# First mixer of a two-block network: order of the weight queue, place of the filters, one accumulating bank for the modulation, low ranks side by side

## The reference

```python
mod_x = split((silu(c) @ w_ada + b_ada), 6)          # 6 x 1024, and mod_c from c_ctx
def project(h, mod):
    p = modulate(rmsnorm(h, norm_mix_g), mod[0], mod[1]) @ w_in
    q, k, v, g, a_f, a_b, hy = split(p)
    la_f = log_sigmoid(a_f @ gla_wa_f + gla_ba_f) / 16   # a_f, a_b: 16 columns each
    la_b = log_sigmoid(a_b @ gla_wa_b + gla_ba_b) / 16
gla_c = project(ctx, mod_c)                          # the context gives states only
gla_x = project(x, mod_x)
_, s_f, s_b = gla_bidir(*gla_c)
o_x = gla_bidir(*gla_x, s_f, s_b)
filt = hyena_filters(hy_w1, hy_b1, hy_w2, hy_b2, hy_w3, hy_freq)
y = concat([gla_out(o_x, g), hyena(hy, hy_conv_w, hy_conv_b, filt, hy_bias)]) @ w_out
x = x + mod_x[2] * y
x = x + mod_x[5] * expert_choice_moe(...)            # experts: 201 MB of weights
```

## Time and profile before

| | |
|---|---|
| median of 3 executions | 1749.27 us (1746.94 to 1749.31) |
| profiled execution | 1747.91 us, span 1746.0 us |
| TensorE busy | 1501.8 us (86%), granted clock 0.936 |
| VectorE, ScalarE busy | 513.7 us (29%), 332.2 us (19%) |
| DMA | 493.45 MB, mean 283 GB/s |

### The profile page before, as it was taken

How to read it: one execution, slowest core, us unless ns; L and a number is a source line. 1 busy time by engine, 2 the same in 40 slices (tenths; PEclk the granted TensorE clock), 3 DMA queues, 4 the chain that set the end, 5 groups by cost and what they waited for, 6 DMA issues and landing times.

```text
span 1746.0 us, 18568 instructions
## 1 busy us (share of the span) xinstructions
PE 1501.8 (86%) x7642; PEld 834.0 (48%) x7642; DVE 513.7 (29%) x1103; ACT 332.2 (19%) x693; POOL 0.2 (0%) x4
## 2 busy tenths in 40 slices
PE   6999998775665666589999899999899998999997
PEld 3567776331221211156778443343567785434434
DVE  6312742100111100015653322121347624221213
ACT  1423211100000000102331322111223323122112
POOL 0000000000000000000000000000000000000000
PEclk9999998888888878889999899999999999999998
DMA  9325528799999999982331699999214216999980
GB/s 387 141 76 203 204 108 374 306 427 427 427 427 429 427 427 429 426 347 99 114 113 55 267 411 394 390 388 391 111 59 183 97 49 241 402 394 402 370 358 26
DMA packets 35309, 493.45 MB, mean 283 GB/s; under 512 B 3920, under 2 KB 4304, under 8 KB 4688
## 3 DMA queue, kind: packets, MB, share of 16 engines
q1 hardware_dynamic: 34784, 491.62, 68.7%
q10 hardware_dynamic: 432, 0.52, 0.1%
HBM read 491.08 MB, written 1.05 MB: 282 GB/s over the span
## 4 chain that ended last, share of the span: by engine, by line
PE 72%; DMA 21%; DVE 4%; ACT 1%; issue 1%; DVEq 0%; ACTq 0%
PE PS L543 22%; DMA A<-ring_d 21%; PE PS L1343 13%; PE PS L1366 7%; PE PS L856 3%; PE PS L1328 3%; PE PS L1216 3%; PE PS L1381 3%; PE PS L548 3%; PE PS L1007 2%; PE PS L1205 1%; PE PS L1042 1%; PE PS L613 1%; PE PS L1169 1%; PE PS L555 1%
## 5 line engine op out<-in xcount | busy, mean ns | idle before, releaser
L543 PE MATMUL PS<-A 128*128 128x256 f32 (+7 forms) x1744 | 424.7, 402 | 7.5 <-ACT A L2363 3.8
L856 PE MATMUL PS<-A 128*32 128x512 f32 x1536 | 237.7, 754 | 154.6 <-DMA A<-ring_d 154.6
L543 PEld LDWEIGHTS PS<-A 128*128 128x128 f32 (+2 forms) x1744 | 313.5, 197 | 107.2 <-issue 59.5
L1343 PE MATMUL PS<-A 128*64 128x512 f32 x1024 | 226.8, 595 | 0.2
L856 PEld LDWEIGHTS PS<-A 128*32 128x32 f32 x1536 | 52.6, 124 | 329.3 <-issue 249.9
L1343 PEld LDWEIGHTS PS<-A 128*64 128x64 f32 x1024 | 71.5, 137 | 133.8 <-issue 132.3
L1366 PE MATMUL PS<-A 128*64 128x512 f32 x512 | 116.9, 598 | 0.0
L1849 DVE TENSOR_TENSOR A<-A,PS 128x512 f32<-128x512 f32 x8 | 5.5, 690 | 344.3 <-PE PS L856 344.3
L548 PE MATMUL PS<-A 128*128 128x128 f32 (+1 forms) x462 | 73.1, 290 | 27.6 <-DVE A L1849 7.1
L548 PEld LDWEIGHTS PS<-A 128*128 128x128 f32 (+1 forms) x462 | 55.8, 150 | 71.5 <-issue 43.1
L2250 DVE TENSOR_TENSOR A<-A,PS 128x256 f32<-128x256 f32 x32 | 13.5, 423 | 225.2 <-ACT A L2782 225.2
(11 more groups left out here) (337 smaller groups left out, 1255.6 us busy)
## 6 DMA issues: line engine op xcount, KB each, us to landing
A<-ring_d SPq DMA_DIRECT2D x228, 2048.0 KB, 12.2
A<-ring_d SPq DMA_DIRECT2D x2, 1312.0 KB, 16.1
A<-ring_d SPq DMA_DIRECT2D x2, 1280.0 KB, 16.6
A<-xT_d SPq DMA_DIRECT2D x2, 1024.0 KB, 9.0
A<-p_d SPq DMA_DIRECT2D x1, 1278.5 KB, 5.5
A<-p_d SPq DMA_DIRECT2D x1, 1232.0 KB, 24.6
A<-pf_d SPq DMA_DIRECT2D x2, 512.0 KB, 13.2
A<-cT_d SPq DMA_DIRECT2D x1, 1024.0 KB, 19.7
```

The lines of the kernel that those rows point to most:

```text
L543: ins = g.matmul(out, l, r, start=n == 0, stop=n == len(pairs) - 1)
L856: ins = g.matmul(ps[32 * e:32 * e + 32, :], rows_of(kk, e), wv[:, kk % 2, e, :], start=kk == 0, stop=kk == 7)
L1343: ins = g.matmul(ps[64 * s:64 * s + 64, :], XS2[u % 2][:, kk, c:c + 64], wv[:, kk % 4, s, :], start=kk == 0, stop=kk == 7)
```

## The change

It does this:
- **Order.** `FILTERS` is split. `SETUP` holds the sine network's first part, the norms, `ada 0` to `3`, `mod 0`, `hm`, and `hz` at its end; the eight `ht` and two `sp` go into the merged strand behind `g 3`. `GLA_IN` begins with `k 1 0`, `k 1 1`. `LATE` has `ada 4` to `11`, and the shares are other.
- **New order** that results: w1 w2 xsq xsum xs, ada 0, csq csum cs, ada 1 to 3, mod 0, hm 1, hm 0, hz, k 1 0, k 1 1, a, gates, k 0 0, k 0 1, v 1 0, b 0 1, ada 4, v 1 1, b 1 1, kt 0 1, ada 5, q 0, st 0 1, q 1, kt 1 1, v 0 0, b 0 0, ada 6, st 1 1, v 0 1, kt 0 0, g 0, ada 7, b 1 0, st 0 0, g 1 to 3, qk 0, kt 1 0, ada 8, ht 0 0 to 1 0, scr 0 0, ht 1 1, st 1 0, ht 1 2, scr 0 1, ht 1 3, sp 0, ada 9, sp 1, hy 0, qk 1, hy 1, ada 10, hy 2, scr 1 0, hy 3, scr 1 1, o 0, ut 0, cv 0, ada 11, o 1, hy 4, osum, hy 5, hy 6, ob 0, ob 1, mod 1, hy 7, ic 0, ut 1, cv 1, hy 8 to 11, ic 1, wr, out 0.
- **Queue.** The constants come in three parts (0.42, 0.56 and 0.51 MB) at three places; the 1 MB of positions is replaced by two small tables that VectorE adds by broadcast; `w3`, decay, and the transform tables are issued later, those of ScalarE's queue now on SP's. The mixer's 20 blocks use three buffers throughout.
- **Modulation.** All blocks of a group add up in one held bank: the coefficients `SCP` are taken at a shifting place, so that block n lands in rows of its own. One copy and four column matmuls end a group.
- **Low ranks.** `a` multiplies both sources in one step, in columns 0 to 48 and 64 to 112 of the array.
- **Smaller.** The sine network's second layer makes 128 rows, and ScalarE a copy with a sign, in place of `wf`; `hm` has 3 rows on ScalarE and 5 on VectorE; the first two operations of `cv` on VectorE are made whole.

The core of the diff:

```diff
-FILTERS = [("w1",), ("w2",), ("hz",), ("xsq",), ("xsum",), ("wf",)] + [("ht", odd, od) for odd in range(2) for od in range(4)] \
-    + [("xs",), ("csq",), ("ada", 0), ("ada", 1), ("csum",), ("cs",), ("sp", 0), ("ada", 2), ("ada", 3),
-       ("mod", 0), ("sp", 1), ("hm", 1), ("hm", 0)]
+SETUP = [("w1",), ("w2",), ("xsq",), ("xsum",), ("xs",), ("ada", 0), ("csq",), ("csum",), ("cs",), ("ada", 1), ("ada", 2), ("ada", 3),
+         ("mod", 0), ("hm", 1), ("hm", 0), ("hz",)]
+FILTERS = [("ht", odd, od) for odd in range(2) for od in range(4)] + [("sp", 0), ("sp", 1)]
-GLA_IN = [("a", 1), ("a", 0), ("gates",)] + [("k", s, j) for s in (1, 0) for j in range(2)]
+GLA_IN = [("k", 1, 0), ("k", 1, 1), ("a",), ("gates",), ("k", 0, 0), ("k", 0, 1)]
-LATE = [("ada", b) for b in range(6, 12)] + [("mod", 1)]
-MIX1 = FILTERS + GLA_IN + merged((REST + CONV, 1), (gla_direction(0), 0.65), (gla_direction(1) + GLA_OUT, 0.65), (LATE, 0.15)) \
+LATE = [("ada", b) for b in range(4, 12)] + [("mod", 1)]
+MIX1 = SETUP + GLA_IN + merged((REST + FILTERS + CONV, 1), (gla_direction(0), 1), (gla_direction(1) + GLA_OUT, 0.8), (LATE, 0.16)) \
...
             def ada(blk):
-                if blk in (0, 4):
-                    fresh("mod", blk // 4 > 0, hold=True)
+                n = int(blk > 3)
+                first, last = ((0, 3), (4, 11))[n]
...
+                c = 14 - 2 * (blk - first)
                 for kk in range(2):
                     for q in range(4):
-                        ins = g.matmul(ps[32 * q:32 * q + 32, :], SCP[:, 2 * q + kk, :], wv[:, 2 * q + kk, :], start=kk == 0, stop=kk == 1)
+                        ins = g.matmul(bank("ada", n)[32 * q:32 * q + 32, :], SCP[:, 2 * q + kk, c:c + 32], wv[:, 2 * q + kk, :],
+                                       start=blk == first and kk == 0, stop=blk == last and kk == 1, skip_group_check=True)
-                if blk not in (0, 4):
-                    mod_columns(blk - 1)
...
-            def a_(s):
-                across(("a", s), w_ab, 0, 49, rows_ready(s))
+            def a_():
+                ps = fresh("a")
+                g.wait_ge(*at("late"))
+                rows_ready(1)
+                rows_ready(0)
+                for k in range(8):
+                    for s, r in ((1, slice(0, 49)), (0, slice(64, 113))):
+                        ins = g.matmul(ps[r, 0:256], w_ab[:, k, :], (H, CH)[s][:, k, :], start=k == 0, stop=k == 7)
...
             def cv(o):
+                v.tensor_tensor(YS[:, 0:2, :], E, XO, ALU.add).then_inc(*out())
+                settle()
+                v.tensor_tensor(YS[:, 2:4, :], E, XO, ALU.subtract).then_inc(*out("cv", o, 0))
...
         def sync(q):
+            constants(1, "in0", "p1")
+            q.dma_start(X, xT_d.rearrange("p (k t) -> p k t", k=8)).then_inc(*land("in2", "in2"))
             for i, (key, n) in enumerate(order):
                 if i == 1:
                     q.dma_start(M, cT_d.rearrange("p (k t) -> p k t", k=8)).then_inc(*land("in3", "ctx"))
+                elif i == 4:
+                    constants(2, "in10", "late")
+                elif i == 5:
+                    q.wait_ge(*at("ch", "n", 1))
+                    tables("w3", w3, "in1", "w3")
+                    q.wait_ge(*at("h", "n", 1))
+                    tables("decay", decay, "in7", "decay")
+                elif i == 6:
+                    constants(0, "in12", "perm")
+                    tables("masks", masks.bitcast(F32), "in6", "masks")
+                    q.dma_start(CE, pf_d[:, PF["CE"][0]:PF["CE"][0] + 128]).then_inc(*land("in4", "CE"))
+                    tables("CF", CF, "in11", "CF")
+                    tables("IC", IC, "in5", "IC")
```

More of the change, by code:

```diff
@@ L46 @@
 ])
-PF, PFN = columns([("decay", 1024), ("w3", 2048), ("CE", 128), ("CF", 512), ("IC", 512), ("mF", 128), ("mB", 128)])
+PF, PFN = columns([("decay", 1024), ("w3", 1024), ("CE", 128), ("CF", 512), ("IC", 512), ("masks", 256)])
 CAP = 128
 CAPX = 64
-COST = dict(ada=4, hy=8, ht=2, sp=8, ut=2, cv=8, ic=2, q=8, k=8, v=16, g=8, csum=8, xsum=8, a=8, b=20, kt=14, st=20, qk=16, scr=4, o=8, osum=10,
+COST = dict(ada=4, hy=8, ht=2, sp=8, ut=2, cv=8, ic=2, q=8, k=8, v=16, g=8, csum=8, xsum=8, a=12, b=20, kt=14, st=20, qk=16, scr=4, o=8, osum=10,
             kx=8, cq=16, ckv=8, cqsum=2, kvsum=1, kpe=2, vm=2, qa=4, km=2, qb=2, ca=16, cb=2, kir=2, vc=13, bkr=1, ix=1, tk=2,
             da=16, db=2, sc=3, sm=3, tr=3, pv=3)
-AFTER = {("ada", 6): ("hy", 0), ("b", 1, 1): ("v", 1, 1), ("o", 0): ("scr", 0, 1)}
+AFTER = {("hy", 0): ("sp", 1), ("b", 1, 1): ("v", 1, 1), ("o", 0): ("scr", 0, 1)}
 for _d in range(2):
@@ L177, with mixer_slots @@
 YE_SLOT, MT_SLOT = 7, 8
-SLOTS = [0, 1, 2, 3] * 2 + [0, 1, 2] * 4 + [4, 5, 6, YE_SLOT, 0, 1, 2, MT_SLOT] + [4, 5, 6, 0, 1, 2] * 14 + [4, 5, 6, 0] \
+def mixer_slots():
+    use = {}
+    for n, (kind, *a) in enumerate(MIX1):
+        key = dict(ada=lambda: ("ada", a[0]), q=lambda: ("qk",), k=lambda: ("qk",), v=lambda: ("v",), g=lambda: ("g",),
+                   hy=lambda: ("hy", a[0] // 4), out=lambda: ("out", a[0] // 2)).get(kind, lambda: None)()
+        if key:
+            use[key] = (use.get(key, (n, n))[0], n)
+    through, slots = [-1] * NM, []
+    for first, last in sorted(use.values()):
+        x = through.index(min(through))
+        assert through[x] < first
+        through[x] = last
+        slots.append(x)
+    in_order = sorted(range(NM), key=lambda x: through[x])
+    return [in_order.index(x) for x in slots]
+SLOTS = mixer_slots() + [4, 5, 6, YE_SLOT, 0, 1, 2, MT_SLOT] + [4, 5, 6, 0, 1, 2] * 14 + [4, 5, 6, 0] \
     + ([1, 2, 4, 5, 0] * 2 + [1, 2, 4, 5, 0, 6] * 8) * 2
@@ L593, in sp @@
                         ins.then_inc(*full("sp", o, x))
[L595 to L601, removed]
             def ada(blk):
-                if blk in (0, 4):
-                    fresh("mod", blk // 4 > 0, hold=True)
+                n = int(blk > 3)
+                first, last = ((0, 3), (4, 11))[n]
                 w, i = weights("ada", blk)
                 wv = w.rearrange("p (k n) -> p k n", k=8)
-                ps = fresh("ada", blk)
+                if blk == first:
+                    fresh("ada", n, hold=True)
+                c = 14 - 2 * (blk - first)
                 g.wait_ge(*at("scp"))
@@ L1563, in xsq @@
                 v.wait_ge(*at("in2"))
-                v.wait_ge(*at("places"))
-                v.tensor_tensor(X, X, T, ALU.add).then_inc(*out("xa"))
+                for k, place, shape in ((0, p1("posr", 4, 4, 1), [128, 4, 4, 64]), (4, p1("posc", 4, 1, 64), [128, 4, 4, 64])):
+                    rows = X[:, k:k + 4, :].rearrange("p k (r c) -> p k r c", r=4)
+                    ins = v.tensor_tensor(rows, rows, bc(place, shape), ALU.add)
+                    ins.then_inc(*(out("xa") if k else out()))
                 settle()
@@ L1630, in ic, with a_ @@
                 v.tensor_tensor(dst, UF[:, m, :], gate_, ALU.mult).then_inc(*out("ic", o, m))
-            def a_(s):
-                full("a", s)
-                v.tensor_scalar(aF[0:49, s, :], bank("a", s)[0:49, 0:256], p1("aone")[0:49, :], None, ALU.add).then_inc(*out("a", s))
+            def a_():
+                v.wait_ge(*at("late"))
+                full("a")
+                for s, r in ((1, slice(0, 49)), (0, slice(64, 113))):
+                    v.tensor_scalar(aF[0:49, s, :], bank("a")[r, 0:256], p1("aone")[r, :], None, ALU.add).then_inc(*out("a", s))
+                note("dve", "a")
             def gates():
@@ L2393, in ada @@
             def ada(blk):
-                full("ada", blk)
-                if blk >= 2:
-                    full("columns", blk - 2)
-                s.activation(ROW[blk % 2], bank("ada", blk), ACT.Copy).then_inc(*out("ada", blk))
+                if blk not in (3, 11):
+                    return
+                n = int(blk > 3)
+                full("ada", n)
+                s.activation(ROW, bank("ada", n), ACT.Copy).then_inc(*out("ada", n))
             def xsq():
```

157 lines of the change are left out of this document (81 added, 76 removed).

## The result

The changed kernel takes 1740.25 us at the median (1736.2 to 1741.9), before 1749.27 (1746.9 to 1749.5): a ratio of 0.9948, 95% interval 0.9934 to 0.9963. That is 9.0 us, where 9.5 were forecast. Its profiled execution took 1740.78 us with a span of 1738.9, 7.1 us under that of before, so 7 us is what the two traces have to explain; the rest of the 9.0 lies in which executions were profiled.

The account below looks back on a forecast made before the run. DMA bounds the setup and first expert stage, TensorE the rest; savings ahead of the first expert block count in full. Front 5.2, low ranks 2.7, modulation 6.4, `wr` 3.6, waits and clock -8.4: 9.5 us, 1739.8; range 1731 to 1747.5.

Parts of the forecast that it names:

- The anchor: Expert stage: it starts from TensorE's first expert block, so 1 us saved ahead should be 1 us at the end.
- The front: Setup up to `k 1 0`: start at 38.4 (bounds 36 and 41) for 58.1; net +5.2 us after filters paid later.
- 1.4 us of slack: Load of the `qk` block ahead of `k 1 0`: landed at 37.0, so the load had 1.4 us to spare.
- the rival of a setup on a low clock: Setup: `csum` and `ada 1` to `3` run low, 7.6 us more, 1747.4 in all; chance 0.07.
- The low ranks: Step `a`: both sources side by side take 3.5 us for 9.7; less 0.8 wait and 2.7 low clock, +2.7 us.
- The price of the rival: Step `a`: the two ranks run in turn, 3.4 us dearer, 1743.2 in all; chance 0.05.
- The modulation's columns: Behind the late `ada` blocks: seven of eight groups of four column matmuls go, 1.0 or 0.9 us each, +6.4 us.
- The waits: TensorE's long stage up to `out 0`: waits in the new order sum to 12.7 us, against 7.0 before.
- The clock: Ahead of `out 0`: three of five waits above 1 us draw low stretches of 2.7 us each, 8.0; bounds 0 to 16.
- the walk through the new order: Stage up to `out 0`: following the new order step by step for waits; last `ic` at 250.5, `out 0` about 251.
- the sum by parts: Whole kernel: 5.2 + 2.7 + 6.4 + 3.6 - 8.4 = 9.5 us saved.
- The rival's break-even: Three buffers too few at `qk` and `ada 5`: gain gone above 12.9 us per load, 3.5 slower from 14.6; chance 0.08.

## Why the prediction was right, and where not

- **The anchor** was right: the DMA-bound stage is as long, the saving at the first expert block (6.9) is that at the end (7.1), and holding the queue back by 12 us costs nothing.
- **The front**: `k 1 0` starts at 38.4, to the tenth as forecast, which is luck (unchanged, it starts anywhere from 36.7 to 39.0), and released by another. I had `qk` asked for at 29.4 and landing by 37.0, with the modulation last. It was asked for at 30.2, took 8.2 us and came last, at 38.38; the modulated rows would have let `k` start 0.7 us earlier. The step "1.4 us of slack" was wrong, and hid because the modulation came out 0.7 us early. `csum`'s second half took 2.66 us, between the 1.9 and 3.8 I gave as bounds; `ada 1` to `3` took 6.3 us, 0.7 over full speed. So the rival of a setup on a low clock was right in kind and far off in size: 1.4 us for the 7.6 it gave. The Trainium skill ("TensorE: Matmul & The Clock Gate", Part 1) says that the throttled clock is the default state and that activity releases it. The trace agrees: `xsum` took 5.5 us, where `csum` did the same work in 3.7 before, and the second half of `csum` 2.66, where the first took 1.99.
- **The low ranks**: `a` took 3.66 us (3.5 forecast), `gates` waited 1.26 (0.8), `k`'s low start cost 2.5 (9.38 for 6.9; 2.7 forecast). Right. The price of the rival was off: in turn they take 2.6 us more, not 3.4.
- **The modulation's columns**: 0.91 us a group, right, shown in the trace; in the medians only partly.
- **`wr`** lies in VectorE's tail ahead of `out 0`, as forecast. It took 1.9 us at the high clock (3.6 before, at a low one), and 1.12 us of wait are left: 3.0 us, where I had 3.6 with `wr` in it.
- **The waits**: nine forecast with 13.5 us (12.7 and the 0.8 of `gates`; `wr` inside the last), the same nine found with 10.7, or 12.6 with the 1.9 of `wr`. `sp 0` was the largest miss (2.3 for 1.16).
- **The clock** is the term that was mis-sized. I gave three low stretches of 2.7 us, 8.0. There were three, but the one behind `o 0` cost 9.1: `o 0` 12.0 us for 6.7, `ut` 2.0 for 1.2, `cv 0` 6.67 for 3.67. With 1.8 behind `osum` (two `hy` in 8.7 us for 6.9) and 1.6 in `cv 1` (5.24 for 3.67) it is 12.5. A row of before gave the price of one stretch, and I took each new one to be as short; this one lasted until about 192, over three steps. Without low clock the walk through the new order had `out 0` at 242.5; 256.3 less 12.5 is 243.8. So the walk was right to 1.3 us, and of the 5.8 us by which `out 0` came behind its 250.5, 4.5 are the clock's. With the measured sizes in it (2.2 for the low ranks, -11.6 for waits and clock), the sum by parts gives 5.8 us at `out 0`, where 5.5 were measured.
- **What makes the sum come out** all the same: the sum by parts, 9.5, was already 1.8 short of the walk's own gain at `out 0` (261.8 - 250.5 = 11.3); 1.4 us came behind `out 0`, from its high clock, which I had left out; and 1.9 us lie between the profiled executions and the medians. That 1739.8 stood for 1740.25 is in part luck: by the traces alone it was 9.5 against 7.1. The next ten executions repeat the gain of the medians, 9.0 us (1747.94 to 1738.94).
- **Three buffers** were enough, as argued: behind `k 1 0` TensorE waits for no block until the experts. The rival's break-even was worked out wrong: with slacks of 1.4 and 0.7 us, loads of 13.4 us eat the 9.5, and loads of 15.2 make it 3.5 us slower, not 12.9 and 14.6.
- **The first expert block** comes 51.3 us behind `out 0`, where the signs to look for had 56. That was counted from `wr` (258.2 to 314.5 before); from `out 0` it was 52.7 before. The sum doesn't use it.

## What to carry to other kernels

A wait of TensorE can have two prices: its own length, and a low clock behind it, which here was more than six times as dear as the wait (9.1 us for 1.39). So when an order is made, a wait like those of `o 0` and `ut 1` should be covered by a step that waits for nothing, and if there is none, by products that nobody reads; check that the next engine in the row doesn't take the time back. It is no full cure: small products behind one another drew a low stretch in `o 1` without a wait, and a wait of `gates`, `osum` or `out 0` had one in some executions and none in others. So price these stretches as a range, and profile more than one execution. Filling the setup's idleness with the first projections and putting off what only a later stage needs was worth all of this change, in this order of the rest; the setup is then bound by the bytes ahead of the first weights.

## What the runs showed of the hardware that I had not expected

- A wait of 1.39 us, behind a microsecond of small products (`scr`), was followed by a granted clock of 0.50 for some 13 to 20 us, though TensorE was busy from its end on but for the 0.78 us ahead of `cv 0`. It became high again in `cv 0`, whose products are 512 columns wide. In the kernel before, the low window at 190 ended after some 8 us with `hy` products in it, and in the kernel with the columns put back the stretch in `o 1` ended in `hy 4` (256 columns). That the small products of `o` kept it low is argued from this, not shown; with the wait filled, the same products ran at 1.00.
- The clock also fell with no wait at all: in both profiles with the columns put back it went to 0.50 in `o 1`, some 11 us after TensorE's last wait had ended, behind a microsecond of products with two columns.
- A wait of 1.16 us ahead of `sp 0` was in none of the 11 profiles that have it followed by a low window, while the one of 1.90 us ahead of `osum` was followed by one in 11 of 12. The one of 1.26 us ahead of `gates` had one in 3 of 10, the one of 1.12 ahead of `out 0` in 1 of 11. The length of a wait alone doesn't tell.
- Behind waits filled with products of a matrix of ones with itself, `k 1 0` and the expert rows ran at 1.00 (3.72 and 3.81 us), where they had run low without (5.38 and 5.63).
